# Eight x buffers, a second DMA queue and a new split of the low halves in the first block of a hybrid decoder layer

## The reference

```python
def hybrid_layer(h, norm_w, w_in, ...):
    u = rmsnorm(h, norm_w)
    proj = jnp.einsum('btd,dc->btc', u, w_in)       # 4104 columns
    hg_q, hg_f, hg_i, hg_z, gd_qkv, gd_z, gd_a, gd_b = jnp.split(proj, ...)
    ...                                             # HGRN2 heads, gated delta-net heads, conv, gates
    return jnp.einsum('btc,cd->btd', y, w_out)

h = jnp.concatenate([meta, x], axis=1)
h = h + hybrid_layer(h, ...)
y = rmsnorm(h, final_norm_w)[:, N_META:]
```

## Time and profile before

| | |
|---|---|
| time, median of 3 runs | 921.14 us (918.52 to 921.93) |
| span of the profiled execution, first to last instruction | 918.0 us |
| TensorE matmul busy | 803.6 us, 88% of the span |
| TensorE weight load busy | 753.3 us, 82% |
| VectorE busy | 482.8 us, 53% |
| GpSimd busy | 341.2 us, 37% |
| ScalarE busy | 320.2 us, 35% |
| DMA queue busy, of 16 engines | 18.7% |
| mean granted TensorE clock | 0.968 |

### The profile page before, as it was taken

The page is one execution under the profiler, slowest core; times in us unless marked ns, Lnnn a source line. Parts: engine busy times, 40 slices in busy tenths (PEclk is TensorE's granted clock), DMA queues, the critical chain, the costliest instruction groups (busy, mean ns, idle before and its releaser), DMA issues. The chain is left out here.

```text
span 918.0 us, 15166 instructions
## 1 busy us (share of the span) xinstructions
PE 803.6 (88%) x5418; PEld 753.3 (82%) x5418; DVE 482.8 (53%) x1052; ACT 320.2 (35%) x835; POOL 341.2 (37%) x458
## 2 busy tenths in 40 slices
PE   2499978999998889999978898999878968999983
PEld 2279978899997789899978898999878967988862
DVE  3454668834333788342336883433368828322237
ACT  3444523333433233325232333352324345411114
POOL 2415356633012566330125662301256526112206
PEclk9999999999999899999998999999989988999987
DMA  2302021022100310110002103300050044125024
GB/s 92 143 4 59 9 69 32 7 41 44 28 1 16 70 38 10 35 44 24 1 22 64 38 10 44 41 17 1 21 73 7 10 140 163 62 94 171 1 96 202
DMA packets 51173, 46.89 MB, mean 51 GB/s; under 512 B 3026, under 2 KB 45844, under 8 KB 51108
## 3 DMA queue, kind: packets, MB, share of 16 engines
q1 hardware_dynamic: 51108, 45.95, 18.7%
HBM read 35.79 MB, written 10.16 MB: 50 GB/s over the span
## 5 line engine op out<-in xcount | busy, mean ns | idle before, releaser
L214 PE MATMUL proj<-uTh,w_high 128*128 128x352 f32 (+1 forms) x768 | 275.4, 359 | 15.9 <-issue 10.6
L214 PE MATMUL proj<-uTh,w_low 128*128 128x352 f32 (+1 forms) x768 | 248.8, 324 | 0.0
L214 PE MATMUL proj<-uTl,w_high 128*128 128x352 f32 (+1 forms) x768 | 248.2, 323 | 0.0
L214 PEld LDWEIGHTS proj<-uTh,w_high 128*128 128x128 f32 x768 | 147.8, 192 | 17.5 <-issue 17.1
L214 PEld LDWEIGHTS proj<-uTl,w_high 128*128 128x128 f32 x768 | 147.7, 192 | 0.0
L214 PEld LDWEIGHTS proj<-uTh,w_low 128*128 128x128 f32 x768 | 146.3, 190 | 0.0
L232 POOL TENSOR_TENSOR w_low<-w_raw,w_high 128x256 fp32r<-128x256 f32 (+1 forms) x66 | 82.2, 1246 | 163.6 <-ACT w_high L224 163.4
L1138 PE MATMUL mix<-level_x 128*128 128x128 f32 x448 | 67.4, 284 | 20.0 <-DVE level_x L994 12.5
L1138 PEld LDWEIGHTS mix<-level_x 128*128 128x128 f32 x448 | 61.0, 195 | 26.6 <-issue 18.9
L1039 DVE SCALAR_TENSOR_TENSOR conv_out<-conv_in,hg_taps,conv_out 128x352 f32<-128x352 f32 (+1 forms) x108 | 75.1, 695 | 1.3
L1549 DVE COPY_PREDICATED gd_n<-mask_ts,mix 128x384 f32<-128x384 uint8 (+1 forms) x60 | 34.4, 572 | 63.5 <-PE mix L1615 61.2
(11 more groups left out here) (288 smaller groups left out, 1466.3 us busy)
## 6 DMA issues: line engine op xcount, KB each, us to landing
w_raw<-in_w_in SPq DMA_DIRECT2D x32, 512.0 KB, 8.6
x_tile<-in_x SPq DMA_DIRECT2D x8, 512.0 KB, 8.5
w_raw<-y_scratch SPq DMA_DIRECT2D x8, 448.0 KB, 4.7
out_y<-w_raw SPq DMA_DIRECT2D x4, 512.0 KB, 2.7
hg_q<-in_w_out SPq DMA_DIRECT2D x2, 512.0 KB, 4.6
hg_th<-in_w_out SPq DMA_DIRECT2D x2, 512.0 KB, 5.3
hg_v<-in_w_out SPq DMA_DIRECT2D x2, 512.0 KB, 6.9
hg_z<-in_w_out SPq DMA_DIRECT2D x2, 512.0 KB, 6.2
```

Source lines behind the costliest of these rows:

```text
L214: last = pe.matmul(acc[:, 0:tw], w[j % 2][:, k, :], u[:, k, t0:t0 + tw], start=(k == 0 and i == 0), stop=(k == KT - 1 and i == 2))
```

## The change

There are eight x buffers and not four, so that SyncE waits for transposes only before x 8. SyncE issues x 1 ahead of the parameter rows, then x 2 to 8, and the second weight tile last. The first weight tile and the gate columns are issued by ScalarE, at the head of its own queue. The low parts of second halves (odd n) move from VectorE to GpSimd, each behind the `rstd` of the following tile, with a semaphore for each of the two engines. VectorE takes the low part of a first half behind the norm of the second half. GpSimd makes the low halves of a weight tile in one go: the first at i = 3, the second after the last tile. The cast of the gate columns moves to i = 4 on ScalarE, their low half to n = 9 on VectorE, the cast of the second weights to i = 8. `BESIDE` is dealt out anew, head 0 ahead of its gate part.

```diff
-    XS = 4
+    XS = 8
...
-    BESIDE = {4: [("gate", 0, range(0, 5))], 5: [("gate", 0, range(5, PARTS))], 6: [("head", 0, range(0, 5))],
-              7: [("head", 0, range(5, PARTS))],
-              NC - 1: [("gate", 1, range(PARTS)), ("head", 1, range(PARTS)), ("gate", 2, range(PARTS))]}
+    BESIDE = {4: [("head", 0, range(0, 5))], 5: [("head", 0, range(5, PARTS)), ("gate", 0, range(0, 2))],
+              6: [("gate", 0, range(2, PARTS))], 7: [("head", 1, range(0, 6))],
+              NC - 1: [("gate", 1, range(PARTS)), ("gate", 2, range(PARTS)), ("head", 1, range(6, PARTS))]}
...
-        cleared, u_high, u_low = sem("cleared"), sem("u_high"), sem("u_low")
+        cleared, u_high = sem("cleared"), sem("u_high")
+        u_low = [sem("u_low_dve"), sem("u_low_pool")]
...
         def _(sp):
+            def load_x(i):
+                sp.dma_start(xt[i % XS][:, :], x[0, (i - 1) * P:i * P, :]).then_inc(x_in[i % XS], 16)
+
             sp.dma_start(xt[0][0:META, :], meta_tokens).then_inc(x_in[0], 16)
+            load_x(1)
             sp.wait_ge(cleared, 1)
...
-            for i in range(1, XS):
-                sp.dma_start(xt[i][:, :], x[0, (i - 1) * P:i * P, :]).then_inc(x_in[i], 16)
-            sp.dma_start(gate_raw[:, :, :], w_in_v[:, :, AB_COLS:AB_COLS + 2 * HEADS]).then_inc(gate_in, 16)
-
-            sp.dma_start(raw[1][:, :, :], tile_cols("hg", 0, 0)).then_inc(raw_loaded[1], 16)
+            for i in range(2, XS):
+                load_x(i)
             for i in range(XS, NC):
                 full(sp, p1, ("x", i - XS, 1))
-                sp.dma_start(xt[i % XS][:, :], x[0, (i - 1) * P:i * P, :]).then_inc(x_in[i % XS], 16)
-                if i == XS:
-                    sp.dma_start(raw[0][:, :, :], tile_cols("hg", 1, 0)).then_inc(raw_loaded[0], 16)
+                load_x(i)
+            sp.dma_start(raw[0][:, :, :], tile_cols("hg", 1, 0)).then_inc(raw_loaded[0], 16)
...
+        def low_part(eng, n):
+            i, half = divmod(n, 2)
+            w = rows_of(i)
+            t0 = 0 if i == 0 else META + (i - 1) * P
+            eng.wait_ge(u_high, n + 1)
+            eng.tensor_tensor(ul[:, 4 * half:4 * half + 4, t0:t0 + w],
+                              ut[n % 3][:, 0:4 * w].rearrange("p (k t) -> p k t", k=4),
+                              uh[:, 4 * half:4 * half + 4, t0:t0 + w].bitcast(F32),
+                              ALU.subtract).then_inc(u_low[n % 2], 1)
...
+            def early_low(n):
+                pool.wait_ge(w_high, n + 1)
+                for k in range(LOW_PARTS):
+                    ks = slice(k * KT // LOW_PARTS, (k + 1) * KT // LOW_PARTS)
+                    last = pool.tensor_tensor(wl[n][:, ks, :], raw[1 - n][:, ks, :],
+                                              wh[n][:, ks, :].bitcast(F32), ALU.subtract)
+                last.then_inc(w_low, 1)
+
             for i in range(NC):
...
-                if i in (3, 4, 6, 7):
-                    n = i // 6
-                    pool.wait_ge(w_high, n + 1)
-                    for k in (2 * (i % 3), 2 * (i % 3) + 1):
-                        ks = slice(k * KT // LOW_PARTS, (k + 1) * KT // LOW_PARTS)
-                        last = pool.tensor_tensor(wl[n][:, ks, :], raw[1 - n][:, ks, :],
-                                                  wh[n][:, ks, :].bitcast(F32), ALU.subtract)
-                    if i % 3:
-                        last.then_inc(w_low, 1)
+                if i:
+                    low_part(pool, 2 * (i - 1) + 1)
+                if i == 3:
+                    early_low(0)
+            low_part(pool, 2 * (NC - 1) + 1)
+            early_low(1)
...
+            act.dma_start(raw[1][:, :, :], tile_cols("hg", 0, 0)).then_inc(raw_loaded[1], 16)
+            act.dma_start(gate_raw[:, :, :], w_in_v[:, :, AB_COLS:AB_COLS + 2 * HEADS]).then_inc(gate_in, 16)
             square_tile(0)
...
-                if i == 1:
+                if i == 4:
                     act.wait_ge(gate_in, 16)
                     act.copy(gate_h[:, :, :], gate_raw[:, :, :]).then_inc(gate_high, 1)
-                if i in (3, 6):
+                if i in (3, NC - 1):
                     act.wait_ge(raw_loaded[1 - i // 6], 16)
                     act.copy(wh[i // 6][:, :, :], raw[1 - i // 6][:, :, :]).then_inc(w_high, 1)
...
             if n >= 3:
-                dve.wait_ge(u_low, n - 2)
+                dve.wait_ge(u_low[(n - 3) % 2], (n - 3) // 2 + 1)
...
                 norm_part(dve, n)
-                if n:
+                if n % 2:
                     low_part(dve, n - 1)
-                if n == 3:
+                if n == 9:
                     dve.wait_ge(gate_high, 1)
...
-            low_part(dve, 2 * NC - 1)
...
-                    pe.wait_ge(u_low, 2 * (1 + -(-(t0 + tw - META) // P)))
+                    for low in u_low:
+                        pe.wait_ge(low, 1 + -(-(t0 + tw - META) // P))
```

More of the change, by code:

```diff
@@ L391, in _ @@
             take_beside(NC - 1)
[L393 to L401, removed]
         def norm_part(dve, n):
```

## The result

The changed kernel takes 934.39 us (median of 4 runs, 932.85 to 935.34); the kernel before, on the same chip, 921.06 us. The ratio is 1.0144, with a 95% interval of 1.0124 to 1.0163: the change makes the kernel 13.3 us slower, where 8.7 us less were forecast. The profiled execution has a span of 932.4 us (918.0 before), and a mean granted clock of 0.965 (0.968).

What follows compares the result with a forecast made beforehand. Late x tiles behind small-piece loads in SyncE's queue bound the first block; its last matmul would end at 55.0, not 64.0 (9.0 us), less 0.3 for contention: gain 8.7, span 909.3, time 912.4 us, range 908.0 to 917.5.

Steps and rivals of the forecast that it cites:

- The start: Loads and parameter chain ahead of the first tile: parameter rows at 4.6 us, first scale at 6.85 and not 8.50.
- nothing at all: What SyncE's and ScalarE's DMA queues do to each other at the start: no hold, the bound taken; the other was a full hold.
- Rival (2): Start of the queue: x 1 and row loads held behind ScalarE's weights and gate columns, 16 us, time 928; chance 0.09.
- The loop: Per-tile chain of norm, high, low part and rstd on GpSimd, scale, norms: 4.96 us per tile.
- Rival (4): The per-tile loop through GpSimd takes 5.5 us, with contention in every low part: gives back 2.7, time 915; chance 0.18.
- The four pieces of the weights: GpSimd's split of the first weights at i = 3, between low (2,1) and rstd (4): 2.8 us.
- TensorE: Its beside-parts start at 27.1 us and not just before 39.25; its last matmul of the block ends at 55.0.
- Low (6,1): Low part of tile 6's second half on GpSimd: ends at 42.0 us, TensorE waiting 1 us for it.
- The 18 matmuls behind it: TensorE's matmuls from 42.1 us, ahead of the transposes of tile 8: 2.9 us.
- The cover of the weights' cast: ScalarE's wait for the first weights at i = 3: reached at 13.5, weights at 13.5 to 15, cover until 15, hidden narrowly.
- contention: GpSimd and VectorE locking each other out in the loop: 0.1 us in three of the tiles, 0.3 in all.

Runs made afterwards that it cites:

- one-queue run: The changed kernel with the first weights and gate columns issued by SyncE behind x 7, nothing by ScalarE: 920.3 us, ratio 1.0001 to the kernel before.

## Why the prediction was wrong

**The start failed**, at the step that put the two queues side by side and took "nothing at all" of the two bounds for what they do to each other. Predicted: rows at 4.6, first scale at 6.85. Measured: 24.13 and 26.37, 19.5 us later. Rival (2) described this: the place (the start of the queue), the mechanism and most of the price (first scale at about 23, time 928, 6.4 us short of the measured one). It had 0.09. Its argument from the trace was stronger than I weighed it: the earlier trace rows already had small pieces going out at 103 to 134 per us, with the DMA engines four fifths idle under the weights, so the limit was not the bytes that they move, and nothing in the rows said that a second queue would lift it. Against the rival I had only that the row was of one queue. Where the limit lies no run shows.

**The loop held.** 4.96 us forecast per tile, 5.0 to 5.1 measured. The group by shape, for the term that no row had:

```profile
L316 POOL TENSOR_TENSOR uTl<-u_part,uTh 128x512 fp32r<-128x512 f32 x8 | 10.3, 1287 | 21.7 <-ACT uTh L362 21.7
```

1.287 us, where I took 1.29 from the earlier trace rows; a straight line between its two rows gives 1.27. Rival (4), 5.5 us, did not come about: low part and VectorE's subtraction met for 0.05 us (49.99 + 0.69 against 50.63). The four pieces of the weights took 2.75 us (2.8 forecast). What I had not asked is whether the loop alone is a loss. It is one, 9.9 us in the kernel before; the 3.06 us that I set beside it was one distance of four, and their mean was 4.1; I had set its cost against a start that I took to be earlier, and the sum hid it.

**TensorE.** 48.1 us were forecast from the first scale to the end of the last matmul, 49.8 measured (26.37 to 76.17). Low (6,1) came 35.7 us after the first scale, 0.5 later than forecast; TensorE was there a little early, so that its wait was 2.1 us instead of 1. The 18 matmuls behind it took 4.5 us instead of 2.9, at the granted clock of 0.55 after that pause: this was the term mis-sized. The transposes and the last 54 matmuls together gave back 0.5; the 54 took 8.6 us as forecast, and the first 15 were 0.29 us apart, where I had 0.30.

**The cover of the weights' cast** (13.5 to 15, "hidden, narrowly") was not tried in the changed kernel, where all was late, and no run has the weights first with the x tiles served beside them. In the two runs that change only the loads and have the early start, the weights stand behind x tiles and the cover fails: in the one-queue run ScalarE stands 7.88 us for them, and with ScalarE's loads behind the rows 3.43 us for them and 4.75 us for the gate columns. The two end at 920.3 and 921.6. So with the start nearly as I had it, my gain of 8.7 us goes there.

**The rest.** From the next block on the changed kernel needs 854.4 us and the kernel before 852.5. It begins that block with 4.5 us at a granted clock of 0.66, where the kernel before has 1.00:

```profile
78.00:82.50 4.50, 4.09 (x22) 4.01 (x23) 3.70 (x22) 1.46 (x2) 2.10 (x8) 0.66 0.18 34
```

That is 22 matmuls against 32, 10 x 0.16 = 1.6 us. But over the profiled executions of all thirteen kernels the rest lies between 850.9 and 855.7 us (860.6 in that of the gate columns as 128 pieces), and the run with low parts on VectorE has 0.62 there and 852.4 us in all of the rest. The four executions of the changed kernel, too, differ by 2.5 us. Why the clock falls at this place in some kernels was not tried.

Sum: 19.5 of the start, 1.65 of TensorE, 1.9 of the rest and 0.4 of the gap between the blocks (1.84 and not 1.46 us), less the 0.3 that I had allowed for contention, is 23.1, the difference of the spans, 932.4 and 909.3. The median lies 2.0 and not 3.1 above the profiled span, and 1.1 less is 22.0, the difference of 934.4 and 912.4.

## What to carry to other kernels

Count a load by its pieces, not only by its bytes: here 1024 pieces held the loads issued behind them for 8 to 11 us, be they of 32 or of 512 B, and a second queue did not let others past (x 6 and x 7 of one run excepted); issue first what is wanted first, the small-piece loads last. Before work is moved to an idle engine, follow what that engine has to deliver next and to whom: if the moved work comes between two links of a chain that runs once per tile, its whole length, with the way there, is added to every tile. Take the parts of a mixed change one by one in the forecast, with a price for each alone, since a gain in one can hide a loss in another.

## What the runs showed of the hardware

ScalarE's queue, with 1024 pieces of 512 B under way (97 per us, 22% of the DMA engines busy), let no piece of SyncE's queue through between 5 and 9 us, yet where several x tiles had been issued ahead of its pieces, both queues moved together from 10 to 15 us (348 packets of one and 358 of the other in 5 us). SyncE's issue of 4 KB took 2.76 to 3.14 us with two loads of small pieces ahead of it, against 0.27 to 0.37 us with none. GpSimd's float32 subtraction took 1.287 us for 512 elements, 2.39 for 1024: 2.5 and 2.3 ns per element. The same 32 KB as 128 pieces instead of 1024 let the rows land 7.9 us earlier.
